# The end of a retention head: readings of the states in one go, norm and product ahead of the second round of updates

## The reference

```python
def retention_block(S, inputs):
    q, k, v = inputs
    ...
    scores = jnp.einsum('bhtd,bhsd->bhts', q, k) * decay
    o = (jnp.einsum('bhts,bhsv->bhtv', scores, v)
         + jnp.einsum('bhtd,bhdv->bhtv', q * q_dec[None, :, :, None], S.astype(v.dtype)))
    S_new = s_dec[None, :, None, None] * S + jnp.einsum('bhsd,bhsv->bhdv', k * k_dec[None, :, :, None], v).astype(S.dtype)
    return S_new.astype(S.dtype), o
...
    yb = rms_norm(o.transpose(0, 2, 1, 3), ret_g).reshape(B, L, B_WIDTH) * jax.nn.silu(zb)
    y = jnp.concatenate([ya, yb], axis=-1) @ w_out
```

## Time and profile before

| | |
|---|---|
| median of 3 runs | 2930.8 us (2925.21 to 2931.32) |
| the profiled execution | 2932.06 us, of which the span is 2930.5 us |
| TensorE busy | 2811.0 us, 96% |
| VectorE busy | 1484.1 us, 51% |
| ScalarE busy | 1083.2 us, 37% |
| GpSimd busy | 562.4 us, 19% |
| mean granted TensorE clock | 0.985 of full |

### The profile page before, as it was taken

The page is one execution under the profiler, slowest core; times in us unless marked ns, Lnnn a source line. Parts: engine busy times, 40 slices in busy tenths (PEclk is TensorE's granted clock), DMA queues, the critical chain, the costliest instruction groups (busy, mean ns, idle before and its releaser), DMA issues. The chain is left out here.

```text
span 2930.5 us, 40758 instructions
## 1 busy us (share of the span) xinstructions
PE 2811.0 (96%) x13344; PEld 2136.8 (73%) x13344; DVE 1484.1 (51%) x2013; ACT 1083.2 (37%) x1439; POOL 562.4 (19%) x669
## 2 busy tenths in 40 slices
PE   6689999999999999999989899999999999999997
PEld 2257778777888888888876577788777867787866
DVE  5775454545444554454446645454545444544544
ACT  5574332434233233233323644243344234332421
POOL 2030003100221111311113302122202320231123
PEclk9999999999999999999999999999999999999999
DMA  8876454656455555555545746554646454655454
GB/s 294 279 241 207 155 180 152 201 163 196 138 178 168 168 169 164 169 162 167 157 153 169 223 128 208 180 180 132 209 152 204 146 183 141 227 155 179 151 185 131
DMA packets 303013, 523.44 MB, mean 179 GB/s; under 512 B 33041, under 2 KB 131473, under 8 KB 301945
## 3 DMA queue, kind: packets, MB, share of 16 engines
q1 hardware_dynamic: 261570, 389.19, 42.1%
q0 software_dynamic: 41280, 132.20, 13.9%
HBM read 460.29 MB, written 60.96 MB: 178 GB/s over the span
## 5 line engine op out<-in xcount | busy, mean ns | idle before, releaser
L969 DVE TENSOR_TENSOR wlo<-raw,whi 128x1024 fp32r<-128x1024 f32 x733 | 900.3, 1242 | 975.3 <-ACT whi L672 971.7
L672 ACT ACTIVATE whi<-raw 128x1024 fp32r<-128x1024 f32 x733 | 769.0, 1057 | 1378.3 <-PE acc L1426 1274.7
L1426 PE MATMUL acc<-whi,hT_hi 128*128 128x512 f32 x2496 | 994.4, 398 | 2.0 <-DVE work L1086 1.2
L1426 PE MATMUL acc<-whi,hT_lo 128*128 128x512 f32 x2496 | 975.2, 391 | 0.0
L1426 PE MATMUL acc<-wlo,hT_hi 128*128 128x512 f32 x2496 | 974.8, 391 | 0.0
L1426 PEld LDWEIGHTS acc<-whi,hT_hi 128*128 128x128 f32 x2496 | 469.9, 188 | 138.3 <-issue 35.9
L1426 PEld LDWEIGHTS acc<-whi,hT_lo 128*128 128x128 f32 x2496 | 469.9, 188 | 100.4
L1426 PEld LDWEIGHTS acc<-wlo,hT_hi 128*128 128x128 f32 x2496 | 470.3, 188 | 94.5 <-issue 1.0
L1426 PE MATMUL acc<-whi,yT_hi 128*128 128x512 f32 x768 | 300.9, 392 | 3.5 <-DVE yT_lo L1095 2.6
L1426 PE MATMUL acc<-wlo,yT_hi 128*128 128x512 f32 x768 | 299.6, 390 | 0.0
L1426 PE MATMUL acc<-whi,yT_lo 128*128 128x512 f32 x768 | 299.5, 390 | 0.0
(11 more groups left out here) (200 smaller groups left out, 1980.2 us busy)
## 6 DMA issues: line engine op xcount, KB each, us to landing
raw<-in_w_in_e SPq DMA_DIRECT2D x448, 256.0 KB, 3.0
raw<-in_w_mod SPq DMA_DIRECT2D x384, 256.0 KB, 3.6
raw<-in_w_in_o SPq DMA_DIRECT2D x384, 256.0 KB, 3.1
out<-state POOLq DMA_DIRECT2D x96, 512.0 KB, 3.5
raw<-in_w_out_e SPq DMA_DIRECT2D x128, 256.0 KB, 3.4
state<-in_state_gla POOLq DMA_DIRECT2D x64, 512.0 KB, 5.2
raw<-in_w_out_o SPq DMA_DIRECT2D x128, 256.0 KB, 3.7
work<-gate_rows POOLq DMA_DIRECT2D x64, 256.0 KB, 4.5
```

The lines of the kernel that those rows point to most:

```text
L672: act.activation(whi[jj][:, :, :], raw[jj][:, :, :], ACT.Copy).then_inc(s["hi_ready"], 1)
L969: dve.tensor_tensor(wlo[jj][:, :, :], raw[jj][:, :, :], whi[jj][:, :, :].bitcast(F32), ALU.subtract).then_inc(s["lo_ready"], 1)
L1426: return pe.matmul(out, lhsT, rhs, start=start, stop=stop, skip_group_check=True)
```

## The change

TensorE reads all four pieces in one go (`ret_read`), behind the second granule of a projection at the place of the first piece, or directly behind the prompt part in the panel; the first round follows it. The second round (`ret_round(before, 2)`) stays behind the fourth granule in a projection, and moves from behind the second to behind the fourth in the panel. There, `turn_out` waits for the first round's updates only. On VectorE the norm moves ahead of the second round's updates in a projection, and ahead of both rounds' updates in the panel, where the second round's updates move to the end. On GpSimd the power comes ahead of all stores, and the products stand between stores 0, 1 and stores 2, 3.

```diff
@@ GpSimd, ret @@
-                for c in range(CH_RT):
+                rsqrt(h + (2 + A_HEADS))
+                for c in range(2):
                     st_store(ret_piece, ret_s[0], h, c, h * CH_RT + c, 4)
-                rsqrt(h + (2 + A_HEADS))
                 pool.wait_ge(s["o_done"], h * NT + NT + LEAD)
                 products(ai + 2, onb, lambda t: wb[:, t, :])
+                for c in range(2, CH_RT):
+                    st_store(ret_piece, ret_s[0], h, c, h * CH_RT + c, 4)
                 st_free(h + 1)
@@ VectorE, out @@
                     if kind == "rt" and before:
+                        ret_norm(before)
                         ret_update(before, 0)
                         ret_update(before, 1)
                     split(r, 1)
-                    if kind == "rt" and before:
-                        ret_update(before, 2)
-                        ret_update(before, 3)
-                        ret_norm(before)
...
                     if kind == "rt" and before:
                         turned(before, 0, True)
                     split(r, 3)
+                    if kind == "rt" and before:
+                        ret_update(before, 2)
+                        ret_update(before, 3)
@@ VectorE, ret @@
                     ret_update(before, 1)
                 split(r, 2)
+                if before:
+                    ret_norm(before)
                 split(r, 3)
                 if before:
                     ret_update(before, 2)
                     ret_update(before, 3)
                 split(r + 1, 0)
-                if before:
-                    ret_norm(before)
@@ TensorE, turn_out @@
-                        pe.wait_ge(s["up_done"], h * (2 * CH_RT) + 2 * CH_RT)
+                        pe.wait_ge(s["up_done"], h * (2 * CH_RT) + (CH_RT if wide else 2 * CH_RT))
@@ TensorE, out @@
                         if g == 0:
                             ret_prompt(before)
-                            ret_pieces(before, 0)
-                        if g == 1:
-                            ret_pieces(before, 2)
+                            ret_read(before)
+                            ret_round(before, 0)
                         if g == 2:
                             turn_out(before, 0, True)
                             turned(before)
+                        if g == 3:
+                            ret_round(before, 2)
@@ TensorE, new functions @@
+            def ret_read(before):
+                h = before[1]
+                for c in range(CH_RT):
+                    pe.wait_ge(st_in[c], h * 16 + 16)
+                for kt in range(KH):
+                    for b in (0, 2, 4, 6, 1, 3, 5, 7):
+                        g0, half = 32 * (b // 2), DVB * (b % 4)
+                        ins = mm(OB[1][g0:g0 + 32, 0:DVB], qmask[:, kt, b, :],
+                                 state[2 * kt + b // 4][:, half:half + DVB], False, kt == KH - 1)
+                ins.then_inc(s["o_full"], 1)
+
+            def ret_round(before, c):
+                h, kt = before[1], c // 2
                 if c:
                     pe.wait_ge(s["up_done"], h * (2 * CH_RT) + 2 * c)
...
@@ TensorE, ret @@
+                def first_round():
+                    ret_read(before)
+                    ret_round(before, 0)
+
                 if before:
-                    project(r, ai, {0: lambda: ret_prompt(before), 1: lambda: ret_pieces(before, 0),
-                                    3: lambda: ret_pieces(before, 2)})
+                    project(r, ai, {0: lambda: ret_prompt(before), 1: first_round, 3: lambda: ret_round(before, 2)})
```

More of the change, by code:

```diff
@@ L1640, in ret_prompt @@
                 pe.wait_ge(s["qm_done"], h + 1)
-            def ret_pieces(before, c):
-                h, kt = before[1], c // 2
[L1646 to L1653, removed]
+            def ret_read(before):
[9 more added lines that the diff above has]
+            def ret_round(before, c):
+                h, kt = before[1], c // 2
                 if c:
```

## The result

The changed kernel takes 2939.93 us, median of 7 runs (2937.47 to 2943.73), beside 2930.4 us for the kernel before (7 runs, 2925.21 to 2932.74). The ratio is 1.0036, with a 95% interval of 1.0025 to 1.0048: 9.5 us slower at the medians, 7 to 14 by the interval. The forecast was 2941.5 and +10.3.

A forecast was written before the change was run, and what follows sets the result against it. TensorE, busy for 96% of the span, was taken as the bound. Seven endings −1.0, head 7's panel +9.7 and the clock in panel 1 +1.6 gave +10.3 us: forecast 2941.5 us, range 2934 to 2947.

The forecast's parts named there:

- The seven endings: Head endings inside the input projections: one reading group saves TensorE 0.15 us each, 1.0 us together, bounds 0 and 2.
- the norm and the later split: VectorE in the seven ordinary endings: split 3 comes about 4 us later, covered by about 8 us of granules; costs nothing.
- Head 7's chain on the engines: First retention output panel: time line from readings through norm, updates, products, stores and gate rows to panel 1; +9.7 us.
- the start of panel 1: TensorE behind panel 0's eviction: forecast at 1546.7 against 1536.99 before, +9.7 us.
- Granule 3: TensorE in panel 0 after the turn: duration taken midway between 5.55 us after the stall and 3.99 without one.
- the gate rows: Panel 0: 5.83 us from the second load's issue to the eviction; low bound 5.0.
- The clock after the long stall: Panel 1, after TensorE stands some 15 us: slower first matmuls add 1.6 us, bounds 0.8 and 3.4.
- The mechanism: GpSimd in panel 0: the wait for all four stores' landing, no longer hidden, holds the gate rows; 5.0 us taken.
- The shorter stall: Rival, panel 0 between granules 2 and 3: the shorter stall sets the end; −5.8 us, 2925; chance 0.10.
- Short landings: Rival: stores land in 3.2 us and gate rows under 5.0, or readings are cheaper; +4 to +6, 2936; chance 0.13.
- the low bound of −1.8 us: Low end of the range for head 7: stores' landing at 3.2 us in place of the 5.0 taken.
- The stalled ordinary endings: Rival, seven projections: the later split makes each wait 1 us; +7 on top, 2948.5; chance 0.09.

The follow-up runs named there:

- Experiment 4: Changed kernel with TensorE and VectorE in the seven projections in the old order (two readings, norm behind the updates), panel as changed; 2947.49 us, ratio 1.0058.
- 2: Changed kernel with TensorE and VectorE in the panel in the old order, GpSimd's order as changed; 2935.99 us, ratio 1.0019.
- 3: Changed kernel with the panel's old order on TensorE and VectorE, and GpSimd's landing wait behind the gate loads; 2933.64 us, ratio 1.0007.
- 8: Changed kernel with the panel's old order on TensorE and VectorE, stores 2 and 3 and the landing wait behind the gate loads; 2930.12 us, ratio 0.9998.
- 10: Kernel before with TensorE's readings in one go and nothing else changed; 2930.31 us, measured once.
- 1: Changed kernel with GpSimd's landing wait moved behind the panel's two gate loads or to the next head's start; 2940.14 us, ratio 1.0029.
- 5: Changed kernel with the last four panels' gate rows in their own place, loaded ahead of stores 2, 3 and the landing wait; 2929.37 us, ratio 0.9995.
- 6: As 5, with panel 0's eviction ahead of updates 2, 3, stores 2, 3 behind the additions to `x`, landing wait later; 2926.11 us, ratio 0.9984.
- 7: As 6, all four stores behind the panel's additions or the projections' products, panel 0's gate loads not awaiting the turn; 2923.81 us, ratio 0.9978.
- 9: As 7, with stores 0 and 1 right behind panel 0's gate loads and only 2 and 3 behind the additions; 2920.46 us, ratio 0.9965.

## Why the prediction was right

**The seven endings** were forecast to save 1.0 us and saved 0.68. A reading group of 32 instructions takes 1.93 us, as worked out; the second piece takes 1.39 from matmul to matmul (1145.66 to 1147.05 at head 3), as worked out. That the norm and the later split cost nothing there held: TensorE has no listed wait in this stretch, before or after. Experiment 4 shows that "nothing" was right for the change as a whole and not for its parts: GpSimd's new order needs the early norm.

**Head 7's chain on the engines** held nearly to the tenth: the norm 4.94 us, updates done at R + 9.65 (forecast 9.5), products done at R + 13.87 (13.8), the stall 2.50 (2.6), the wait from store 3 to the first gate load 4.87 (5.0), panel 1 at R + 38.44 (38.4).

**Two of its terms were off and cancelled.** That the start of panel 1 was met to 0.01 us is luck. Granule 3 took 6.18 us from its first to its last matmul (1520.56 to 1526.74), where I took 4.77 and had put the bound at 5.55: the clock fell in spite of the shorter stall, with ten slow steps against seven before. Against that the gate rows took 4.85 us from the second issue and not 5.83, less than the 5.0 that I had as a bound: TensorE stood, and the weight loads rested with it, which may be why; no run tells that apart. The bound came from four loads; over all 32 second gate loads of the kernel before, the landing took 4.4 to 9.1 us. The two errors were +1.4 and −1.0 us, and the turn gave back most of the rest (2.44 us from it to granule 3 instead of 2.71).

**The clock after the long stall** cost 1.45 us by the stretch from the first to the last eviction, where I had 1.6. That it came so near is luck too. The profiles have these slow steps, with what TensorE did ahead of them:

| TensorE stood | slow steps behind it |
|---|---|
| 6.42 us at the turn, 1.17 behind it | granule 3: 7 (before), 8 (2), 8 (3), 7 (8), 14 (10) |
| 2.50 us at the turn, 1.2 to 1.3 behind it | granule 3: 10 (after), 11 (1), 7 (4), 13 (5), 10 (6) |
| no stall at the turn, 1.31 behind it | granule 3: 0 (7), 0 (9) |
| 12.4 to 14.4 us ahead of panel 1 | panel 1: 7 (after), 12 (1), 13 (4) |
| 3.2 to 6.6 us ahead of panel 1 | panel 1: 10 (2), 7 (3), 7 (5) |

So one profile's count is a draw from 7 to 14, whether TensorE had stood for 2.5 or for 6.4 us. In experiment 4, after a stall of 14.27 us, the stretch between the evictions was 2.8 us longer than before and not 1.45. Two readings of the prediction don't stand: that the shorter stall would cost less of granule 3, and that a single stall of 6.42 us gives the price of the next one. Its bounds for the clock in panel 1, 0.8 and 3.4, hold all three long stalls; its bound of 5.55 us for granule 3 does not hold (5.59 to 6.70 after the short stall).

**The mechanism** was named as one, GpSimd's wait for the stores' landing. The runs show two that overlap: that wait (4.1 us of idle), and the stores in front of the gate rows. Experiment 1 takes the wait away and gets half of it back at the eviction; 8 and 9 show that the position of the stores in the queue decides. The cause behind both is one order: stores 2 and 3 ahead of the gate loads, at a point where nothing is left to hide them. How the transfer engines share the stores' packets and the gate rows' is not settled by these runs; I only compared orders.

**The rivals.** The shorter stall was real and set nothing. Its condition, gate rows at hand in time, is what experiment 5 supplies, and there R to panel 0's eviction is 1.1 us shorter than before. Short landings did come: stores 2 and 3 landed 3.4 and 3.8 us from their issue, near the 3.2 of that rival. But the next load still went out only 4.87 us behind store 3, so the low bound of −1.8 us put the landing in the place of a term that holds more than the landing. The gate rows were short as well, and the slow granule 3 ate that. The stalled ordinary endings did not come.

## What to carry to other kernels

When a store is moved behind something, follow the queue that issues it down to the next load that someone waits for: a wait for the landing that cost nothing while a norm and a product hid it, together with the stores themselves, cost 9.7 us at the next panel here. Merely moving the wait isn't enough: the small load issued behind stores took 6.8 to 12.0 us, and 4.7 to 5.8 without them. Put the small load that is waited for ahead of the large stores, if need be in a place of its own in memory. And where two profiles differ in stretches that no edit touched, compare the stretches that were touched, not the spans. A cost of the clock that is read from one dip of one profile can be off by a factor of two.

## What the runs showed that was not expected

Time from the issue of the second gate load (256 KB) to the eviction that waits for it, in the output panels behind head 7: 4.69 to 4.85 us with stores landed and TensorE standing (changed, 2, 4), 5.57 to 5.84 with weight loads going and no store under way in front (before, 6, 7, 8, 9, 10), 6.82 behind two stores of 512 KB, 8.41 with four stores issued in the 7.6 us ahead, 12.0 directly behind four in panel 1. Stores issued right behind it did not lengthen it (5.57 in 8, 5.81 in 9).

The Trainium skill's page "DMA: Bandwidth & Descriptors" (section "Anatomy of one DMA") gives one price by size for such a transfer, by its fit an estimate of 2.6 us for 256 KB; no load that the eviction waited for came under 4.69 here, and the shortest landing of any second gate load in these traces is 4.2.

A stall of TensorE of 2.50 us at the turn was followed by as many slow steps as one of 6.42: 7 to 13 against 7 to 14. Without that stall, with only 1.31 us of waiting behind the turn (7 and 9), the granted clock stayed at 1.00.
